# Splitting expert weights in three units of 2048 columns a block in place of six of 1024

## What is computed

```python
def hierarchical_moe(h, w_rg, b_rg, w_re, b_re, w_gate, w_up, w_down):
    ...
    # 32 experts, 2 chosen for each token; w_gate, w_up: (32, 1024, 256), w_down: (32, 256, 1024)
    hg = jnp.einsum('td,edf->tef', t, w_gate)
    hu = jnp.einsum('td,edf->tef', t, w_up)
    act = jax.nn.silu(hg) * hu * combine[:, :, None]
    y = jnp.einsum('tef,efd->td', act, w_down)
    return y.reshape(b, s, d)
```

## Time and profile before

| | us |
|---|---|
| median of 3 runs | 1366.41 (1366.08 to 1367.22) |
| span of the profiled execution | 1363.2 |
| TensorE busy in it | 1309.7 |
| VectorE busy in it | 1032.2 |
| ScalarE busy in it | 872.8 |
| expert stage, first to last matmul of it | 1028.3 to 1344.6 |

### The profile page before, as it was taken

How to read it: one execution, slowest core, us unless ns; L and a number is a source line. 1 busy time by engine, 2 the same in 40 slices (tenths; PEclk the granted TensorE clock), 3 DMA queues, 4 the chain that set the end, 5 groups by cost and what they waited for, 6 DMA issues and landing times.

```text
span 1363.2 us, 23818 instructions
## 1 busy us (share of the span) xinstructions
PE 1309.7 (96%) x9405; PEld 1202.4 (88%) x9405; DVE 1032.2 (76%) x1535; ACT 872.8 (64%) x1289; POOL 78.2 (6%) x81
## 2 busy tenths in 40 slices
PE   7999999999999999999999899999998999999994
PEld 7989999998999998999999888999986777777773
DVE  6776655568555568998998886874569999999994
ACT  6565444546444546675656766654457999999994
POOL 0001000001000000000001100110000111011113
PEclk9999999999999999999999999999999999999997
DMA  8644555553655544555435534454436999999963
GB/s 276 205 152 130 191 185 185 185 186 94 202 185 187 187 140 145 178 161 158 150 102 181 193 122 155 155 186 161 157 156 254 365 360 354 351 366 365 362 261 123
DMA packets 150108, 279.78 MB, mean 205 GB/s; under 512 B 13721, under 2 KB 122238, under 8 KB 136574
## 3 DMA queue, kind: packets, MB, share of 16 engines
q1 hardware_dynamic: 141952, 269.97, 57.0%
q0 software_dynamic: 7696, 8.41, 2.0%
q10 hardware_dynamic: 366, 0.12, 0.0%
HBM read 274.26 MB, written 21.50 MB: 217 GB/s over the span
## 4 chain that ended last, share of the span: by engine, by line
PE 75%; DVE 15%; ACT 5%; issue 3%; DMA 1%; ACTq 0%; DVEq 0%; POOLq 0%; POOL 0%; SPq 0%
PE psum L852 18%; PE psum L854 18%; PE psum L853 18%; DVE weights_parts L2692 3%; PE psum L1413 3%; PE psum L1412 3%; PE psum L1411 3%; DVE weights_parts L2086 2%; PE psum L1437 2%; DVE arena L2476 2%; PE psum L1439 2%; PE psum L1438 2%; ACT weights_parts L1933 1%; ACT weights_parts L1476 1%; PE psum L1256 1%
## 5 line engine op out<-in xcount | busy, mean ns | idle before, releaser
L2086 DVE TENSOR_TENSOR weights_parts<-ring,weights_parts 128x1024 fp32r<-128x1024 f32 (+3 forms) x312 | 363.4, 1184 | 161.5 <-ACT weights_parts L1476 161.1
L1476 ACT ACTIVATE weights_parts<-ring 128x1024 fp32r<-128x1024 f32 (+3 forms) x312 | 309.0, 1010 | 175.6 <-PE psum L854 174.8
L852 PE MATMUL psum<-xnorm_parts,weights_parts 128*128 128x256 f32 x884 | 255.5, 289 | 6.0 <-DVE xnorm_parts L2235 2.0
L853 PE MATMUL psum<-xnorm_parts,weights_parts 128*128 128x256 f32 x884 | 249.0, 282 | 0.0
L854 PE MATMUL psum<-xnorm_parts,weights_parts 128*128 128x256 f32 x884 | 248.9, 282 | 0.0
L852 PE MATMUL psum<-expert_cols,weights_parts 128*128 128x256 f32 (+1 forms) x688 | 194.7, 283 | 3.3 <-DVE expert_cols L2104 2.0
L854 PE MATMUL psum<-expert_cols,weights_parts 128*128 128x256 f32 (+1 forms) x688 | 192.1, 279 | 0.0
L853 PE MATMUL psum<-expert_cols,weights_parts 128*128 128x256 f32 (+1 forms) x688 | 191.9, 279 | 0.0
L852 PE MATMUL psum<-hidden_parts,weights_parts 128*128 128x256 f32 x640 | 181.9, 284 | 2.6 <-DVE hidden_parts L2544 1.7
L853 PE MATMUL psum<-hidden_parts,weights_parts 128*128 128x256 f32 x640 | 180.5, 282 | 0.0
L854 PE MATMUL psum<-hidden_parts,weights_parts 128*128 128x256 f32 x640 | 180.5, 282 | 0.0
(11 more groups left out here) (422 smaller groups left out, 2528.3 us busy)
## 6 DMA issues: line engine op xcount, KB each, us to landing
expert_raw<-in_w_exp_down SPq DMA_DIRECT2D x35, 1024.0 KB, 7.6
ring<-in_mlp_w_up SPq DMA_DIRECT2D x32, 1024.0 KB, 5.4
ring<-in_mlp_w_down SPq DMA_DIRECT2D x32, 1024.0 KB, 4.9
ring<-in_w_in SPq DMA_DIRECT2D x30, 1024.0 KB, 5.3
ring<-in_w_exp_gate SPq DMA_DIRECT2D x23, 1024.0 KB, 5.0
ring<-in_w_exp_up SPq DMA_DIRECT2D x23, 1024.0 KB, 7.3
ring<-in_attn_w_qkv SPq DMA_DIRECT2D x12, 1024.0 KB, 8.4
expert_raw<-in_w_exp_gate SPq DMA_DIRECT2D x12, 1024.0 KB, 5.0
```

The lines of the kernel that those rows point to most:

```text
L852: pe.matmul(out, lh, rh, start=start, stop=False, **more)
L853: pe.matmul(out, lh, rl, start=False, stop=False, **more)
L1476: ins = act.activation(high, src, ACT.Copy)
L2086: ins = dve.tensor_tensor(low, src, high.bitcast(F32), ALU.subtract)
```

## The change

The six units of a block become three of 2048 columns: u = 0 and 1 of gate and up, u = 2 all of down. Three buffers of twice the size take the place of six, in the same memory. ScalarE and VectorE make one instruction where they made two in a row, TensorE signals `unit_used` after 12 matmuls where it did after 6, and all waits count in the new units. `down` waits once for its unit. In the last block a semaphore of its own, `last_half`, tells ScalarE that a half of the result is ready, which `unit_used` did.

```diff
-UNITS_KEPT = 6
+UNITS_KEPT = 3
+WIDE = 2 * UNIT
...
     for n in range(NB + 1):
         if n < NB:
-            order += [(n, u) for u in range(4)]
+            order += [(n, 0), (n, 1)]
         if n:
-            order += [(n - 1, 4), (n - 1, 5)]
+            order.append((n - 1, 2))
...
-        unit_bufs = [moe_units[:, 2 * UNIT * i:2 * UNIT * (i + 1)] for i in range(2)]
-        unit_bufs += [w_parts[:, 2 * UNIT * i:2 * UNIT * (i + 1)] for i in range(UNITS)]
+        unit_bufs = [moe_units[:], w_parts[:, 0:2 * WIDE], w_parts[:, 2 * WIDE:4 * WIDE]]
...
             i = UNIT_NO[n, u]
-            high, low = (unit_bufs[i % UNITS_KEPT][:, h * UNIT:(h + 1) * UNIT] for h in range(2))
-            if u >= 4:
-                return i, down_raw[n % 2][:, (u - 4) * UNIT:(u - 3) * UNIT], high, low
-            src = pair_raw[n % 3][:, :, u * UNIT // 2:(u + 1) * UNIT // 2]
+            high, low = (unit_bufs[i % UNITS_KEPT][:, h * WIDE:(h + 1) * WIDE] for h in range(2))
+            if u == 2:
+                return i, down_raw[n % 2], high, low
+            src = pair_raw[n % 3][:, :, u * WIDE // 2:(u + 1) * WIDE // 2]
...
-                    low_ready(sp, UNIT_NO[n - 3, 3])
+                    low_ready(sp, UNIT_NO[n - 3, 1])
...
-                    low_ready(sp, UNIT_NO[n - 2, 5])
+                    low_ready(sp, UNIT_NO[n - 2, 2])
...
-                    for k in range(2):
-                        kk = 2 * u + k
+                    for k in range(4):
+                        kk = 4 * u + k
...
                 last = n == NB - 1
+                i, _, high, low = unit_views(n, 2)
+                low_ready(pe, i)
+                high, low = (t.rearrange("p (k c) -> p k c", k=2) for t in (high, low))
                 for first, second in ((0, 0), (0, 1), (1, 0), (1, 1)):
                     half, k = (first, second) if last else (second, first)
-                    i, _, high, low = unit_views(n, 4 + k)
-                    low_ready(pe, i)
...
-                    if second == 1:
-                        mm.then_inc(s["unit_used"], 1)
+                    if last and second == 1:
+                        mm.then_inc(s["last_half"], 1)
+                if not last:
+                    mm.then_inc(s["unit_used"], 1)
...
                 if n < NB:
-                    gate_up(n, (0, 1))
+                    gate_up(n, (0,))
                 if n:
                     turn_act(n - 1)
                 if n < NB:
-                    gate_up(n, (2, 3))
+                    gate_up(n, (1,))
...
-            for i in range(2):
-                unit_high(i)
+            unit_high(0)
...
-                unit_highs(2 if n < NB else 0)
+                unit_highs(1 if n < NB else 0)
                 if n:
                     act_high(n - 1)
                 if n < NB:
-                    unit_highs(2)
+                    unit_highs(1)
                     silu(n)
...
                 if n:
-                    unit_highs(2)
+                    unit_highs(1)
...
-                if j in (1, 2):
-                    unit_low(j - 1)
+                if j == 1:
+                    unit_low(0)
...
             window_low(0, columns[0])
+            unit_low(1)
+            window_low(1, columns[1])
             unit_low(2)
-            unit_low(3)
-            window_low(1, columns[1])
-            unit_low(4)
-            unit_low(5)
...
-                unit_lows(2 if n < NB else 0)
+                unit_lows(1 if n < NB else 0)
                 if n:
                     act_low(n - 1)
                 if n < NB:
-                    unit_lows(2)
+                    unit_lows(1)
                     gated(n)
...
                 if n:
-                    unit_lows(2)
+                    unit_lows(1)
```

More of the change, by code:

```diff
@@ L502, in build_two_blocks @@
             "sorted_low", "windows_ready", "window_high", "window_low", "ids_ready", "places_ready", "more_ready",
-            "silu_done", "act_done", "act_full", "act_high", "act_low", "y_copied", "final_sums", "final_root",
+            "silu_done", "act_done", "act_full", "act_high", "act_low", "y_copied", "last_half", "final_sums", "final_root",
             "final_ready", "before_ready", "nat_copied",
@@ L1430, in down @@
                 last = n == NB - 1
+                i, _, high, low = unit_views(n, 2)
+                low_ready(pe, i)
+                high, low = (t.rearrange("p (k c) -> p k c", k=2) for t in (high, low))
                 for first, second in ((0, 0), (0, 1), (1, 0), (1, 1)):
                     half, k = (first, second) if last else (second, first)
-                    i, _, high, low = unit_views(n, 4 + k)
-                    low_ready(pe, i)
                     a_high, a_low = acts[:, n % 2, 0, k, :], acts[:, n % 2, 1, k, :]
                     y, cc = bank(4 + 2 * (n % 2) + half), slice(half * 512, (half + 1) * 512)
-                    pe.matmul(y, a_high, high[:, cc], start=(k == 0), stop=False)
-                    pe.matmul(y, a_low, high[:, cc], start=False, stop=False)
-                    mm = pe.matmul(y, a_high, low[:, cc], start=False, stop=(k == 1))
-                    if second == 1:
-                        mm.then_inc(s["unit_used"], 1)
+                    pe.matmul(y, a_high, high[:, k, cc], start=(k == 0), stop=False)
+                    pe.matmul(y, a_low, high[:, k, cc], start=False, stop=False)
+                    mm = pe.matmul(y, a_high, low[:, k, cc], start=False, stop=(k == 1))
+                    if last and second == 1:
+                        mm.then_inc(s["last_half"], 1)
+                if not last:
+                    mm.then_inc(s["unit_used"], 1)
             for n in range(NB + 1):
                 if n < NB:
-                    gate_up(n, (0, 1))
+                    gate_up(n, (0,))
                 if n:
@@ L1930, in unit_high @@
                     act.wait_ge(pair_in[n % 3], 32 * (n // 3 + 1))
-                if u == 4:
+                if u == 2:
                     act.wait_ge(down_in[n % 2], 16 * (n // 2 + 1))
                 act.activation(high, src, ACT.Copy).then_inc(s["unit_high"], 1)
-            for i in range(2):
-                unit_high(i)
+            unit_high(0)
             for half in range(2):
@@ L1960, in _ @@
             act.activation(std_col[:, 0, 0:1], eps_col[:, 0:1], ACT.Exp)
-            for i in range(2, UNITS_KEPT):
+            for i in range(1, UNITS_KEPT):
                 unit_high(i)
@@ L1973, in window_high @@
                 if n >= 2:
-                    act.wait_ge(s["unit_used"], UNIT_NO[n - 2, 3] + 1)
+                    act.wait_ge(s["unit_used"], UNIT_NO[n - 2, 1] + 1)
                 at = first_column(n) if at is None else at
@@ L1979, in silu @@
             def silu(n):
-                act.wait_ge(s["unit_used"], UNIT_NO[n, 3] + 1)
+                act.wait_ge(s["unit_used"], UNIT_NO[n, 1] + 1)
                 if n >= 2:
@@ L1989, in act_high @@
                 if n >= 2:
-                    act.wait_ge(s["unit_used"], UNIT_NO[n - 2, 5] + 1)
+                    act.wait_ge(s["unit_used"], UNIT_NO[n - 2, 2] + 1)
                 act.activation(acts[:, n % 2, 0, :, :].rearrange("p k t -> p (k t)"), bank(2 + n % 2)[:, 0:2 * P],
@@ L1994, in copy_y @@
             def copy_y(n):
-                act.wait_ge(s["unit_used"], UNIT_NO[n, 5] + 1)
+                act.wait_ge(s["unit_used"], UNIT_NO[n, 2] + 1)
                 if n >= 2:
@@ L2007, in copy_last_y @@
                 for half in range(2):
-                    act.wait_ge(s["unit_used"], UNIT_NO[n, 4 + half] + 1)
+                    act.wait_ge(s["last_half"], half + 1)
                     act.activation(y_rows[:, n % 2, half * 512:(half + 1) * 512], bank(4 + 2 * (n % 2) + half),
@@ L2797, in window_low @@
                 if n >= 2:
-                    dve.wait_ge(s["unit_used"], UNIT_NO[n - 2, 3] + 1)
+                    dve.wait_ge(s["unit_used"], UNIT_NO[n - 2, 1] + 1)
                 at = first_column(n) if at is None else at
```

## The result

The changed kernel takes 1423.66 us (median of 4 runs, 1422.44 to 1425.48) against 1366.24 for the kernel before: a ratio of 1.0427, with a 95% interval of 1.0414 to 1.0439. It is 57 us slower, and 1422 had been predicted.

The account below looks back on a forecast made before the run. The loop of waits through `act_low` was to bound the kernel: start 1043.3, 33 blocks of 10.55 and 1.7 small work gave 1393.2, 55.8 us more; span 1419.0 plus 3.2 gave 1422 us, range 1408 to 1432.

Parts of the forecast that it names:

- The loop by way of `act_low`: Expert stage, from one `down` to the next through TensorE, ScalarE and VectorE: 10.55 us a block against 8.92.
- Durations of the wide instructions: One instruction of 2048 columns in the expert stage: 1.93 us on ScalarE, 2.28 on VectorE.
- ScalarE's loop in second place: ScalarE's waits by way of `down`'s unit and `copy_y`: 7.78 us against 7.84 in the main loop, just behind it.
- Start: Up to the first `down`'s first matmul, D(0): 1043.3 us against 1042.79, 0.5 us more.
- Busy shares: Expert stage after the change: VectorE at 83%, ScalarE at about 80%, DMA at about 0.8.
- The block before: One block of the unchanged expert stage, first `down` matmul to the next: 8.92 us.
- Small work on VectorE: `late_rows`, `mixing_weights` and `spare_blocks` between units on VectorE: 0.66, 0.82 and 0.2 us, 1.7 together.
- Rival 3: TensorE's clock falls through idling 1.65 us in every block: 4.7 us more a block, 1577 us; chance 3%.
- From span to time: Whole run: the median lies 3.2 us above the profiled span, so 1419.0 becomes 1422 us.
- Fewer instructions win (rival 1): Expert stage: fixed costs bound a block, so three fewer VectorE instructions save 8 us, giving 1358 us; chance 3%.
- TensorE's own time: TensorE's own work in a block of the expert stage: 8.9 us, so it stands still for 1.65.

Follow-up runs that it names:

- e1: Changed kernel with `act_low` moved in front of the next block's `unit_low` on VectorE alone: 1359.39 us.
- e3: Changed kernel with `act_high` on ScalarE and `act_low` on VectorE both moved in front of the next block's unit: 1358.35 us.
- e4: Changed kernel with each `unit_high` and `unit_low` made as two instructions of 1024 columns, a signal for each half, release unchanged: 1395.89 us.
- e7: Kernel before with only the release made coarse: `unit_high` of both units of a pair waits until both units in their buffers are used: 1396.29 us.
- e2: Changed kernel with `act_high` moved in front of the next block's `unit_high` on ScalarE alone: 1460.79 us.
- e8: e2 with six matmuls of zeros added in the gap before each `down`: 1439.03 us.
- e10: Changed kernel with six matmuls of zeros in the gap before each `down`, run beside the changed kernel on one chip: 1422.47 us.
- e6: Kernel before with `act_low` moved in front of the next block's two `unit_low` on VectorE alone: 1354.51 us.

## Why the prediction was right, step by step

- *What bounds it.* The loop by way of `act_low` was the right one: 10.54 a block against 10.55, all its points within 0.05 us. e1 and e3 remove it by order alone, e4 and e7 shorten it by the amounts worked out.
- *Durations of the wide instructions.* 1.918 and 2.292 us against 1.93 and 2.28, so the line through 512 and 1024 columns (rows 7) holds at 2048.
- *ScalarE's loop in second place.* 0.06 us behind by the sum, 0.08 in the trace.
- *Start.* D(0) at 1043.21, 1043.3 predicted. Executions differ more than that in when they reach it (1043.2 to 1046.4 in the changed kernel and those made from it), so the closeness is partly luck. In the traces of e1, e2, e3, e4 and e8 one more fall of the clock lies between 1029 and 1042 us, which is one source of this; another lies before the stage, whose first matmul comes at 1028.0 to 1031.0.
- *Busy shares.* 83% and 80% predicted for VectorE and ScalarE in the stage, 79% and 76% measured; DMA 0.80 as predicted. They are no term of the sum.
- *The block before.* The 8.92 of the prediction is one of two alternating blocks, 8.87 is their mean. The sum does not use it, since it sets D(33) against D(33). That of the kernel before was taken from the chain (1337.35 in rows 9); the timeline has 1337.27, 0.08 less.
- *Small work on VectorE.* 1.7 us predicted. In e10, where the clock does not fall, D(1) and D(2) come 0.71 and 0.77 later than a quiet block (0.66 and 0.82 predicted), and rounds 8 to 15 add seven times 0.07 and once 0.14 where I had 0.2: 2.1 together.
- *The clock.* Rival 3 was given 3% as all or nothing, with the gap of a quiet block, 1.65 us. For those blocks it was right to dismiss it: no fall came after any of the gaps of 1.65 to 1.72. Its one counterexample was a gap of 1.5 us, though, and said nothing of longer ones. The step that failed is that I added the small work to the loop and did not see that it makes TensorE's gap 2.4 us in these blocks. Three falls cost 4.5 us of the stage, the longer operation 0.3, and the span became 1423.7 and not 1419.0.
- *From span to time.* I added 3.2, the difference between the median shown and one execution's span. The profiled execution of the changed kernel has 1.8. So 4.7 us too little in the span and 1.4 too much around it, with a median 1.8 below the profiled run, come to 1.5, and to the 1.7 by which the rounded forecast was low. The closeness of the total is in part luck; that of the block is not.
- *Fewer instructions win (rival 1).* The fixed costs were saved: one wide instruction takes 0.07 us less than two in a row on VectorE (2.36 to 2.29) and 0.08 less on ScalarE (2.00 to 1.92). The Trainium skill (Perfetto Trace Analysis, section Optimizing Scalar/DVE Operations) puts this overhead at about 0.06 and 0.093 us, which the traces bear out within 0.015. But with the loop cut both e3 (wide instructions) and e6 (narrow ones) take 8.61 us a block, TensorE's own pace, so that the six instructions saved a block on ScalarE and VectorE bring nothing. e3 is 3.8 us slower than e6 as a whole; of this 1.1 lies between D(0) and D(33) (286.7 against 285.6), and the rest before D(0), where e3's trace has a fall of the clock in the stage and e6's has none, or in what executions differ by.
- *TensorE's own time.* Put at 8.9, it is 8.6. It stood in no term of the sum, only in the size of the gap and in what I expected of e1, e3 and e6, which all came out lower.

## What to carry to other kernels

Joining two instructions saves their fixed cost, but it delays both the release of the buffer upstream and the start of the engine downstream, and on a loop through three engines both come out in the time of a block, less what an engine was late anyway (0.88 of 1.4 us, and 0.79, here), however high the busy shares are; so write down the loop of waits before and after, and sum it. If a short operation on the critical path (`act_low`, 0.42 us) stands in an in-order queue behind a long one that is needed only later, move it in front: that took 0.8% off the kernel before. Ask first what it waits for itself, since the same move on ScalarE, where its input comes later, cost 37 us (16.6 by the loop, the rest by the clock).

## What the runs showed of the hardware

- *TensorE's clock in short gaps.* The granted clock fell from its full level (2.4 GHz) to the lower (1.2 GHz) in or just before `down` after gaps of 2.07 to 2.44 us in the changed kernel, and never after 1.65 to 1.72. The length of the gap alone does not decide it: in e2, 15 of 34 gaps of 2.13 to 2.42 us brought a fall, among them one of 2.13 and not the one of 2.38, and gaps of 2.05 to 2.15 at the start of the stage brought one in five traces (e1, e2, e3, e4, e8) and none in the other seven. Each fall in `down` cost 1.5 us. Six matmuls of zeros in the gap (1.3 us) kept it up, which gained 21.8 us in e2. The Trainium skill (TensorE: Matmul & The Clock Gate, section HAM oscillation) describes a loop in which TensorE's waits lower its clock again and again; e2, with its 15 falls, agrees.
- *The price of a short wait on TensorE.* In the kernel before, `down`'s first matmul came 0.1 to 0.2 us late after the wait for `act_low` and the next one 0.1 later still; with the wait gone (e6) a block takes 8.61 us against 8.87.
